# Moving slot products, a gather and the sort behind the products that free weight tiles (one-core mixture-of-experts layer)

## Chip, cores and metric

One core of one Trainium2 chip runs the whole layer in one program. The metric is the device time of one execution in microseconds. The kernel before takes 644.44 us, the median of three runs (643.93 to 645.47).

## What is computed

The reference is one layer of a trunk for 128 context tokens and 128 latent tokens: a mixer of attention and mLSTM heads, and then a mixture of 64 experts of which each token takes 8. Only the second half matters here:

```
gate   = one_hot(top-8 of 64 experts) * normalised sigmoid scores     # per token
a      = silu(t @ w_gate[e]) * (t @ w_up[e])                          # 1024 -> 256, each expert
routed = sum over e of (a * gate[e]) @ w_down[e]                      # 256 -> 1024
y      = x + g2 * (routed + shared expert)
```

All in float32. The weights of one expert are three matrices of 1 MB, and all 64 experts are read: 192 tiles of 1 MB, most of the 252.55 MB that the kernel moves.

## The kernel before

**Stages.** Up to about 160 us the kernel computes modulation, projections, attention, the mLSTM and the output projection. Then it normalises, scores the experts, and starts on the experts at about 180 us. The experts are what the change is in.

**Experts.** Each expert has 64 slots for tokens (32 for those with few tokens). A step takes two experts (PAIR) or four (QUAD) whose slots fill 128 rows, and a group is two steps, called par 0 and par 1. `two_steps` writes the work of PE for a group, in this order:

1. `gate_up` of par 0 (line 1265): slots times `w_gate` of the step, then times `w_up`, into bank 6.
2. `combine` (L1282) of the step before: its expert outputs are added to the tokens.
3. `activations_turned` (L1348): the product is transposed, DVE copies it to `actT` (L2313).
4. `slots_to_tokens` (L1245), here "slot product": two small matrix products that tell for each slot its token and its gate. DVE's `turned` (L2303, L2305) takes them over into `ptone` and `gslot` and signals `t_copied`.
5. `down` of par 0 (L1341): `actT` times `w_down`, in two halves, into banks 5 and 4. ACT (`yhi`, L1740) and DVE (`ylo`, L2325) empty them.
6. `gate_up` of par 1, then `combine` of par 0.
7. The next group's tokens are gathered in four products (`gather`, L1236, quarters q 0 to 3) into banks 7, 4, 5, 7. ACT copies each to `xe` (L1722, `gathered`) and signals `x_copied`. The transposes of par 1 stand behind the first quarter.
8. The slot product of the next group's par 0 into bank 6, then `down` of par 1.

Before it writes banks 5 and 4, `down` of par 1 waits until the third quarter has been copied out of bank 5 (`x_copied` of `group * 4 + 7`).

In the first group the sort of the experts by their number of tokens is added. `turn_slots` (L1356 to L1360) finds the order, SP reads it before the tiles from the third group on, and `sort_slots` (L1366) permutes the slot tables, which `sorted_out` on DVE takes over. The sort stands between the slot product and `down` of par 0.

**Weight tiles.** The 192 tiles are loaded by SP's queue in one fixed order, each into a place that an earlier tile leaves. There are 16 places, one of them used once, so that tile number g waits for the tile 15 or so before it. SP waits for a semaphore that PE sets at the end of a product: `gate_used` (after the product with `w_gate`), `e_filled` (after `w_up`), `y_filled` (after the second half of `down`). In what follows:

- tiles 19 and 20 wait for `down` of step 0,
- tiles 25 and 26 for `down` of step 1,
- tiles 27 to 30 for the products with `w_gate` and `w_up` of step 2,
- tiles 33 and 34 for the gates of step 3, tiles 35 and 36 for its `w_up`,
- tiles 37 and 38 for `down` of step 3,
- tiles 39 to 42 for the gates of step 4, the first QUAD step.

The groups are PAIR, PAIR, then twice (QUAD, four times PAIR), then QUAD.

The waits in `down` and `gate_up`, and the order at the end of a group:

```
pe.wait_ge(x_copied, group * 4 + (3 if opening else 4))   # gate_up, par 0
pe.wait_ge(t_copied, n + 1)
...
pe.wait_ge(a_copied, n + 1)                               # down, first half
if par == 1 and not last:
    pe.wait_ge(x_copied, group * 4 + 7)
```

Of the kernel before, what the change touches and what calls it, by code (L numbers as in the profile page):

```python
# [14 lines left out]
P = 128  # L15
NST = 2
# [28 lines left out]
PAIR, QUAD = 2, 4  # L45
# [44 lines left out]
def build(nc, t, o, overflow_at=CAP):  # L90

    ctx = ExitStack()
    with ctx:
# [200 lines left out]
        sil = sb("sil", [P, FE], where=late)  # L294
        act_e = sb("act_e", [P, FE], where=late)
        actT = sb("actT", [P, JF, 2 * CAP], where=late)
        over_y = ExitStack()
        slots_turned = sb("slots_turned", [NE, 4, P], where=over_y)
        over_y.close()
        over_y = ExitStack()  # L300
        over_yhl = sb("over_yhl", [P, EW], where=over_y)
        over_y.close()
# [178 lines left out]
            return unit + par if kind == QUAD else unit  # L481

        FIRST_BANKS = (7, 0, 3, 4)
        G2_BANKS = ((7, 4), (4, 5))
        FINAL = (slice(512, 1024), slice(256, 512), slice(0, 256))
        FINAL_BANK = (5, 4, 7)
# [331 lines left out]
        def _(pe):  # L818
# [418 lines left out]
                                 pone[:, s, :, :].rearrange("p a b -> p (a b)"), start=(i == 0), stop=(i == 3))  # L1237
                ins.then_inc(x_filled, 1)

            def slots_to_tokens(kind, par, e, gates):  # L1240

                ps = bank[6 - 2 * par]
                for s in range(NST):
                    one = pone[:, s, 2 * par:2 * par + 2, :].rearrange("p a b -> p (a b)").bitcast(F32)
                    ins = mm(ps[:, 0:2 * kind], one, gates[:, s, bass.ds(e, kind), :].rearrange("p e a -> p (e a)"),  # L1245
                             start=(s == 0), stop=(s == 1))
                ins.then_inc(t_filled, 1)

            def gate_up(kind, par, n, unit, group, again, spread=False):

                w = P // kind
                opening = not again and unit == 0
                if par == 0:
                    pe.wait_ge(x_copied, group * 4 + (3 if opening else 4))
                    pe.wait_ge(t_copied, n + 1)
                for part in range(2):
                    for j in range(kind):
                        weights_ready(pe, kind, par, part, j, unit, again)
                    for k in range(KD):
                        if opening and par == 0 and part == 0 and k == 6:  # L1260
                            pe.wait_ge(x_copied, group * 4 + 4)
                        for j in range(kind):
                            weights = weights_of(kind, par, part, j, unit, again).rearrange("p (k f) -> p k f", k=KD)
                            slots = slice(par * P + j * w, par * P + (j + 1) * w)
                            ins = mm(bank[6][j * w:(j + 1) * w, part * FE:(part + 1) * FE], xe[:, k, slots],  # L1265
                                     weights[:, k, :], start=(k == 0), stop=(k == KD - 1))
                    ins.then_inc((gate_used, e_filled)[part], 1)
                    if spread and part == 0:
                        pe.wait_ge(g2_biased, 1)
                        pe.wait_ge(y_lo, n * 2)  # L1270
                        spread_g2(1)
                        spread_g2(0)
# [96 lines left out]
            def two_steps(kind, e, n, group, unit, following, gates=gate_s, before=True, starts=False, shared=None, ends=False,  # L1369
                          again=False):  # L1370

                last = following is None
                gate_up(kind, 0, n, unit, group, again)
                if before:
                    combine(1, n - 1, more=int(again))
                if starts:
                    turn_slots()
                activations_turned(n)
                slots_to_tokens(kind, 1, e + kind, gates)
                if starts:  # L1380
                    sort_slots()
                down(kind, 0, n, unit, group, last, again)

                if shared == "gate":
                    shared_gate()
                elif shared == "rest":
                    shared_up()
                gate_up(kind, 1, n + 1, unit, group, again, spread=ends)
                if starts:
                    pe.wait_ge(sorted_ready, 1)  # L1390
                    pe.wait_ge(cnt_ready, 1)
                combine(0, n, starts, halves=(0,) if ends else (0, 1), more=int(again))
                if shared == "gate":
                    pe.wait_ge(sg_copied, 1)
                elif shared == "rest":
                    pe.wait_ge(sact_ready, 1)
                if not last:
                    gather(0, group + 1)
                activations_turned(n + 1)
                if ends:  # L1400
                    combine(0, n, halves=(1,))
                if not last:
                    for q in range(1, 4):
                        gather(q, group + 1)
                if shared == "rest":
                    shared_down()
                pe.wait_ge(a_copied, n + 2)
                if not last:
                    slots_to_tokens(following, 0, e + 2 * kind, gate_s)
                if ends:  # L1410
                    down_final(unit)
                else:
                    down(kind, 1, n + 1, unit, group, last, again)

            def first_round():
                gather_first()
                evacuated(pe, "counts")
                gather(2, 0)
                pe.wait_ge(gate_ready, 1)
                pe.wait_ge(token_ids, 2 * NST)  # L1420
                slots_to_tokens(PAIR, 0, 0, gate)
                gather(3, 0)
                two_steps(PAIR, 0, 0, 0, 0, PAIR, gates=gate, before=False, starts=True)
                two_steps(PAIR, 4, 2, 1, 1, QUAD)
                for it in range(TURNS):
                    two_steps(QUAD, 24 * it + 8, 10 * it + 4, 5 * it + 2, 6 * it + 2, PAIR, shared=("gate", "rest")[it])
                    for i in range(4):
                        two_steps(PAIR, 24 * it + 16 + 4 * i, 10 * it + 6 + 2 * i, 5 * it + 3 + i, 6 * it + 4 + i,
                                  PAIR if i < 3 else QUAD)
                two_steps(QUAD, NE - 8, STEPS - 2, GROUPS - 1, NE // 4 - 2, None, ends=True)  # L1430
# [25 lines left out]
        def _(act):  # L1456
# [268 lines left out]
            def pair(par, n_pair, group, last=False, starts=False, ends=False, more=0):  # L1725
                act.wait_ge(e_filled, n_pair + 1)
                A(sil[:, :], bank[6][:, 0:FE], ACT.Silu).then_inc(e_silu, 1)  # L1727
                if starts:
                    act.wait_ge(turns_filled, 1)
                    A(slots_turned[:, :, :].rearrange("p a b -> p (a b)"), bank[1][0:NE, :], ACT.Copy).then_inc(turns_copied, 1)  # L1730
                if par == 1 and not last:
                    gathered(group + 1)
                if ends:
                    for i in range(N_FINAL):
                        act.wait_ge(y_filled, n_pair * 2 + (i + 1))
                        A(act_e[:, :] if i == 2 else final_y(yhi, i), final_out(i), ACT.Copy, scale=gslot[:, par:par + 1]).then_inc(y_hi, 1)
                    return
                for i, n in enumerate((1, 0)):
                    act.wait_ge(y_filled, n_pair * 2 + (i + 1) + more)
                    A(yhi[:, n, :], bank[4 + n][:, :], ACT.Copy, scale=gslot[:, par:par + 1]).then_inc(y_hi, 1)  # L1740

            def shared_gate():

# [48 lines left out]
        def _(dve):  # L1792
# [503 lines left out]
                V.tensor_copy(gate_s[:, :, :, 0], bank[0][:, 2 * NE:4 * NE].rearrange("p (s e) -> p s e", s=NST)).then_inc(sorted_ready, 1)  # L2296
                dve.wait_ge(sorted_ready, 1)

            def turned(kind, par, n):

                ps, w = bank[6 - 2 * par], P // kind
                dve.wait_ge(t_filled, n + 1)
                V.tensor_scalar(ptone[:, par, :], iota[:, :], ps[:, 1:2], None, ALU.is_equal)  # L2303
                for j in range(kind):
                    ins = V.tensor_copy(gslot[j * w:(j + 1) * w, par:par + 1], ps[j * w:(j + 1) * w, 2 * j:2 * j + 1])  # L2305
                ins.then_inc(t_copied, 1)
# [52 lines left out]
                                ALU.mult).then_inc(sact_ready, 1)  # L2359

            def first_round():
                turned(PAIR, 0, 0)
                two_steps(PAIR, 0, 0, PAIR, starts=True)
                two_steps(PAIR, 4, 2, QUAD)
                for it in range(TURNS):
                    two_steps(QUAD, 24 * it + 8, 10 * it + 4, PAIR, shared=(it == 1))
                    for i in range(4):
                        two_steps(PAIR, 24 * it + 16 + 4 * i, 10 * it + 6 + 2 * i, PAIR if i < 3 else QUAD)
                two_steps(QUAD, NE - 8, STEPS - 2, None, ends=True)
# [75 lines left out]
```

## Time and profile before

| | |
|---|---|
| median of three runs | 644.44 us (643.93 to 645.47) |
| span of the profiled execution | 642.9 us |
| median less span | 1.5 us |
| PE busy | 580.9 us (90%) |
| DVE, ACT, POOL busy | 209.8, 168.1, 33.6 us |
| DMA | 252.55 MB, mean 393 GB/s |
| mean granted clock of TensorE | 0.975 |

The profiled execution's own time is known by its span alone, from its first instruction to its last. The times of the three runs lie 1.0 to 2.6 us above this span. Busy shares are means over stages with different limits, and PE's ends are modelled, so a busy PE says little about what bounds a stage.

### The profile page before, as it was taken

Reading aid. Unit: us, or ns where it says so; the run is one execution under the profiler, and the core shown is the slowest. Engines: PE = TensorE matmul, PEld = TensorE weight load, DVE = VectorE, ACT = ScalarE, POOL = GpSimd, SP = SyncE. Lnnn points to the kernel's source line nnn. Section 1 sums busy time; section 2 is a strip of 40 time slices with the busy share of each in tenths; the row PEclk is TensorE's granted clock in tenths of the full one; section 3 lists DMA queues with packets and bytes.
Section 4 is the critical chain, followed back from the end, with each engine's and each line's share of the span. In section 5 each row is a group of like instructions: output and inputs, shape, how many; then the busy total and the mean of one; then the engine's idle time right before and its main releaser. Section 6 shows DMA issues by size and latency. Waiting matters only on the chain.

```text
span 642.9 us, 11139 instructions
## 1 busy us (share of the span) xinstructions
PE 580.9 (90%) x4568; PEld 405.9 (63%) x4568; DVE 209.8 (33%) x474; ACT 168.1 (26%) x309; POOL 33.6 (5%) x79
## 2 busy tenths in 40 slices
PE   0789999999999999989999999587999999998785
PEld 0478777788867676656675757354567676765352
DVE  0287867787832212011212222020121212121103
ACT  3164726672622121111121212010212121212111
POOL 1240210010100000000000000000000000000002
PEclk9989999999999999999999999788999999999879
DMA  8999599989999899999999999999999999999994
GB/s 334 385 339 392 208 363 383 411 317 396 420 378 374 365 415 411 422 422 420 420 421 422 420 420 421 421 422 421 420 422 421 419 421 421 421 421 420 421 399 168
DMA packets 50662, 252.55 MB, mean 393 GB/s; under 512 B 5912, under 2 KB 11680, under 8 KB 26288
## 3 DMA queue, kind: packets, MB, share of 16 engines
q1 hardware_dynamic: 48240, 246.37, 94.5%
q0 software_dynamic: 1840, 4.21, 2.0%
q10 hardware_dynamic: 528, 1.21, 0.5%
q8 instruction: 38, 0.62, 0.4%
q14 instruction: 16, 0.13, 0.1%
HBM read 250.06 MB, written 1.72 MB: 392 GB/s over the span
## 4 chain that ended last, share of the span: by engine, by line
PE 63%; DMA 28%; SPq 3%; ACT 2%; DVE 2%; issue 1%; POOL 0%; POOLq 0%; DVEq 0%; ACTq 0%
PE bank L1265 22%; PE bank L1341 11%; DMA spare<-in_w_up 7%; PE bank L1236 6%; PE bank L1282 5%; DMA xn<-in_w_up 4%; DMA gb<-in_w_down 4%; DMA ring<-in_w_up 4%; DMA ring<-in_w_in 4%; DMA ring<-in_w_mod 2%; PE bank L834 2%; SPq L617 2%; PE bank L876 2%; PE bank L884 2%; PE bank L880 2%; DMA ccol<-in_c 2%
## 5 line engine op out<-in xcount | busy, mean ns | idle before, releaser
L1265 PE MATMUL bank<-ring,xe 128*64 128x256 f32 (+1 forms) x1680 | 179.4, 398 | 22.9 <-DMA ring<-in_w_up 8.2
L1265 PEld LDWEIGHTS bank<-ring,xe 128*64 128x64 f32 (+1 forms) x1680 | 118.0, 131 | 79.3 <-issue 44.8
L1341 PE MATMUL bank<-ring,actT 128*64 128x512 f32 (+1 forms) x368 | 83.6, 617 | 4.2 <-DVE actT L2313 2.1
L2311 DVE TENSOR_TENSOR act_e<-bank,sil 128x256 f32<-128x256 f32 x26 | 11.0, 424 | 188.2 <-ACT sil L1727 188.2
L2325 DVE SCALAR_TENSOR_TENSOR ylo<-bank,gslot,yhi 128x512 fp32r<-128x512 f32 x50 | 37.5, 750 | 83.6 <-ACT yhi L1740 83.6
L1740 ACT ACTIVATE yhi<-bank,gslot 128x512 fp32r<-128x512 f32 x50 | 34.4, 688 | 116.1 <-PE bank L1341 116.1
L1727 ACT ACTIVATE sil<-bank 128x256 f32<-128x256 f32 x26 | 10.0, 385 | 192.1 <-PE bank L1265 192.1
L1236 PE MATMUL bank<-pone,hhi 128*128 128x256 f32 x200 | 50.0, 288 | 0.0
L1341 PEld LDWEIGHTS bank<-ring,actT 128*64 128x64 f32 (+1 forms) x368 | 24.5, 132 | 39.2 <-issue 38.9
L1236 PE MATMUL bank<-pone,hlo 128*128 128x256 f32 x200 | 48.9, 282 | 0.0
L1722 ACT ACTIVATE xe<-bank 128x512 f32<-128x512 f32 x50 | 29.9, 598 | 48.2 <-PE bank L1236 48.2
L1282 PE MATMUL bank<-yhi,ptone 128*128 128x512 f32 x100 | 42.2, 422 | 0.0
L1282 PE MATMUL bank<-ylo,ptone 128*128 128x512 f32 x100 | 39.5, 395 | 0.0
L1236 PEld LDWEIGHTS bank<-pone,hhi 128*128 128x128 f32 x200 | 38.2, 191 | 0.6
L1236 PEld LDWEIGHTS bank<-pone,hlo 128*128 128x128 f32 x200 | 38.1, 191 | 0.6
L1265 PE MATMUL bank<-xn,xe 128*64 128x256 f32 (+1 forms) x160 | 37.9, 392 | 0.0
L1341 PE MATMUL bank<-gb,actT 128*32 128x512 f32 (+1 forms) x56 | 28.8, 662 | 2.1 <-DMA ring<-in_w_down 2.1
L808 POOL TENSOR_TENSOR xn<-xn,xt 128x512 f32<-128x512 f32 (+1 forms) x4 | 4.3, 1106 | 464.5 <-DVE xn L2389 464.5
L1282 PEld LDWEIGHTS bank<-yhi,ptone 128*128 128x128 f32 x100 | 18.7, 187 | 13.1 <-issue 9.8
L1265 PE MATMUL bank<-spare,xe 128*64 128x256 f32 (+1 forms) x112 | 27.0, 397 | 0.0
L445 DVE TENSOR_TENSOR w_rest_over<-ring,w_upper_over 128x4096 fp32r<-128x4096 f32 (+1 forms) x6 | 24.6, 4093 | 7.4 <-ACT w_upper_over L1515 6.0
L876 PE MATMUL bank<-w_upper_over,xhi 128*128 128x512 f32 (+1 forms) x96 | 24.3, 402 | 2.8 <-ACT w_upper_over L1548 2.5
(375 smaller groups left out, 792.0 us busy)
## 6 DMA issues: line engine op xcount, KB each, us to landing
ring<-in_w_gate SPq DMA_DIRECT2D x55, 1024.0 KB, 24.1
ring<-in_w_up SPq DMA_DIRECT2D x50, 1024.0 KB, 25.8
ring<-in_w_down SPq DMA_DIRECT2D x46, 1024.0 KB, 25.8
ring<-in_w_mod SPq DMA_DIRECT2D x12, 2048.0 KB, 13.7
ring<-in_w_in SPq DMA_DIRECT2D x5, 2048.0 KB, 16.1
gb<-in_w_down SPq DMA_DIRECT2D x7, 1024.0 KB, 25.9
gb<-in_w_up SPq DMA_DIRECT2D x5, 1024.0 KB, 21.5
xn<-in_w_gate SPq DMA_DIRECT2D x5, 1024.0 KB, 17.0
```

What stands on the lines that cost most here:

```text
L445: eng.tensor_tensor(proj_rest(c), proj_weights(c), proj_upper(c).bitcast(F32), ALU.subtract).then_inc(first_rest if c == 1 else w_rest, 1)
L617: ins = sp.dma_start(tile(PLACE[g]).rearrange("p (j n) -> p j n", j=JF)[:, :, w], down_dram[e].rearrange("p (j n) -> p j n", j=JF)[:, :, w])
L834: ins = mm(ps[r:r + P // CT, 0:MW], csil[:, CT * a + k, :], w[:, k, MW * c:MW * c + MW], start=(a == 0 and k == 0), stop=(a == 1 and k == ...
L876: mm(ps[s][:, 0:w], xhi[:, k, s * P:s * P + P], proj_upper(c)[:, k, :], start=(k == 0), stop=False)
L880: mm(ps[s][:, 0:w], xlo[:, k, s * P:s * P + P], proj_upper(c)[:, k, :], start=False, stop=False)
L1236: ins = mm(ps[:, k * 256:k * 256 + 256], h[:, s, 2 * q + k, :], pone[:, s, :, :].rearrange("p a b -> p (a b)"), start=(i == 0), stop=(i == 3))
L1265: ins = mm(bank[6][j * w:(j + 1) * w, part * FE:(part + 1) * FE], xe[:, k, slots], weights[:, k, :], start=(k == 0), stop=(k == KD - 1))
L1282: ins = mm(acc[s][n][:, :], ptone[:, par, s * P:s * P + P], y[:, n, :], start=(first and y is yhi), stop=False, skip_group_check=True)
L1341: ins = mm(bank[4 + h][j * w:(j + 1) * w, :], actT[:, f, j * w:(j + 1) * w], weights[:, f, 512 * h:512 * h + 512], start=(f == 0), stop=(f ...
L1722: A(xe[:, 2 * q:2 * q + 2, :], bank[(7, 4, 5, 7)[q]][:, :].rearrange("p (a b) -> p a b", a=2), ACT.Copy).then_inc(x_copied, 1)
L1740: A(yhi[:, n, :], bank[4 + n][:, :], ACT.Copy, scale=gslot[:, par:par + 1]).then_inc(y_hi, 1)
L2325: V.scalar_tensor_tensor(out=ylo[:, n, :], in0=bank[4 + n][:, :], scalar=gslot[:, par:par + 1], in1=yhi[:, n, :].bitcast(F32), op0=ALU.mul ...
```

## The change

Four moves, all in the expert part:

- **First slot product.** In the first group it stood between gathers q=2 and q=3, ahead of the first gates. It now stands behind the products with `w_gate` of step 0 and writes bank 2. The wait for `t_copied` moves to the front of the first `down`.
- **Sort.** `sort_slots` moves from ahead of the first `down` to behind it. Its table `slots_turned` now lies in the place of `sact`, so that it outlives the first `yhi`.
- **Next group's slot product** moves from ahead of `down` of par 1 to behind it.
- **Fourth gather** (q=3) moves behind that slot product. ACT copies it after both `yhi`. The next gates start on three quarters and wait for the fourth at k=6.

DVE's order is unchanged, so that `turned` of the next group stands ahead of both `ylo` of par 1 as before.

```diff
-        over_y = ExitStack()
-        slots_turned = sb("slots_turned", [NE, 4, P], where=over_y)
-        over_y.close()
+        slots_turned = sact[0:NE, :, :].rearrange("p j (a q) -> p (j a) q", a=2)
...
             def gate_up(kind, par, n, unit, group, again, spread=False):
                 if par == 0:
-                    pe.wait_ge(x_copied, group * 4 + (3 if opening else 4))
-                    pe.wait_ge(t_copied, n + 1)
+                    pe.wait_ge(x_copied, group * 4 + 3)
+                    if not opening:
+                        pe.wait_ge(t_copied, n + 1)
...
-                        if opening and par == 0 and part == 0 and k == 6:
+                        if par == 0 and part == 0 and k == 6:
                             pe.wait_ge(x_copied, group * 4 + 4)
...
+                    if opening and par == 0 and part == 0:
+                        pe.wait_ge(gate_ready, 1)
+                        pe.wait_ge(token_ids, 2 * NST)
+                        evacuated(pe, "hb1_0")
+                        slots_to_tokens(PAIR, 0, 0, gate, opening=True)
...
                 if starts:
+                    pe.wait_ge(t_copied, n + 1)
+                down(kind, 0, n, unit, group, last, again)
+                if starts:
                     sort_slots()
-                down(kind, 0, n, unit, group, last, again)
...
                 if not last:
-                    for q in range(1, 4):
+                    for q in range(1, 3):
                         gather(q, group + 1)
                 if shared == "rest":
                     shared_down()
                 pe.wait_ge(a_copied, n + 2)
-                if not last:
-                    slots_to_tokens(following, 0, e + 2 * kind, gate_s)
                 if ends:
                     down_final(unit)
                 else:
                     down(kind, 1, n + 1, unit, group, last, again)
+                if not last:
+                    slots_to_tokens(following, 0, e + 2 * kind, gate_s)
+                    gather(3, group + 1)
...
                 if par == 1 and not last:
-                    gathered(group + 1)
+                    gathered(group + 1, range(3))
...
                     A(yhi[:, n, :], bank[4 + n][:, :], ACT.Copy, scale=gslot[:, par:par + 1]).then_inc(y_hi, 1)
+                if par == 1 and not last:
+                    gathered(group + 1, (3,))
```

**At a group's end.** PE's rows at the end of the first group, of the kernel before. Bank 7 takes the fourth quarter, L1245 is the slot product, L1341 `down`, L1265 the next gates:

```order
L1236 MATMUL bank7<-pone,hhi 128x256
L1236 MATMUL bank7<-pone,hlo 128x256
L1245 MATMUL bank6<-gate_s,pone 128x4 x2
L1341 MATMUL bank5<-ring,actT 64x512 x4
L1341 MATMUL bank4<-ring,actT 64x512 x4
L1265 MATMUL bank6<-xn,xe 64x256
```

The same place in the changed kernel (line 1236 is 1235 there, 1245 is 1244, 1341 is 1346):

```order
L1235 MATMUL bank5<-pone,hhi 128x256
L1235 MATMUL bank5<-pone,hlo 128x256
L1346 MATMUL bank5<-ring,actT 64x512 x4
L1346 MATMUL bank4<-ring,actT 64x512 x4
L1244 MATMUL bank6<-gate_s,pone 128x4 x2
L1235 MATMUL bank7<-pone,hhi 128x256
L1235 MATMUL bank7<-pone,hlo 128x256
```

`down` now follows directly on the third quarter, whose bank 5 it writes. The slot product and the fourth quarter stand between `down` and the next gates.

**The sort.** PE's rows around `down` of step 0, before (L1348 are the transposes, L1366 is `sort_slots`):

```order
L1348 MATMUL bank6<-ident,act_e 128x128 x2
L1245 MATMUL bank4<-gate,pone 128x4 x2
L1366 MATMUL bank0<-place,slots_turned 128x64 x4
L1341 MATMUL bank5<-ring,actT 64x512 x4
L1341 MATMUL bank4<-ring,actT 64x512 x4
```

And changed:

```order
L1353 MATMUL bank6<-ident,act_e 128x128 x2
L1244 MATMUL bank4<-gate,pone 128x4 x2
L1346 MATMUL bank5<-ring,actT 64x512 x4
L1346 MATMUL bank4<-ring,actT 64x512 x4
L1371 MATMUL bank0<-place,sact 128x64 x4
```

Only the slot product is left between the transposes and `down`, and the sort stands ahead of the gates of step 1.

## Rows read from the trace of the kernel before

**Rows 1.** The page, part 2: the span in 40 equal slices.
```profile
GB/s 334 385 339 392 208 363 383 411 317 396 420 378 374 365 415 411 422 422 420 420 421 422 420 420 421 421 422 421 420 422 421 419 421 421 421 421 420 421 399 168
```

**Rows 2.** Stretches: length, busy us of engines, granted clock, DMA share, GB/s.
```profile
180.00:245.00 65.00, 64.69 (x532) 42.85 (x531) 14.24 (x38) 12.72 (x22) 0.00 (x0) 1.00 0.93 381
245.00:300.00 55.00, 50.03 (x471) 33.34 (x465) 10.13 (x25) 8.05 (x14) 0.00 (x0) 1.00 1.01 421
445.00:576.00 131.00, 129.94 (x946) 87.50 (x940) 25.50 (x60) 23.65 (x40) 0.00 (x0) 0.99 1.01 421
```

**Rows 3.** Stretches of 1 us in the opening, the same columns.
```profile
194.00:195.00 1.00, 1.00 (x12) 0.67 (x10) 1.00 (x3) 0.00 (x0) 0.00 (x0) 1.00 0.66 115
195.00:196.00 1.00, 1.00 (x14) 0.64 (x12) 0.73 (x2) 0.00 (x0) 0.00 (x0) 1.00 0.91 385
...
242.00:243.00 1.00, 1.00 (x24) 0.65 (x20) 0.05 (x1) 0.00 (x0) 0.00 (x0) 1.00 0.73 238
```

**Rows 4.** Timeline of SP: start us, us, issue of a tile (19, 25, 37, 39).
```profile
193.17 0.33 SPq L546 DMA_DIRECT2D ring<-in_w_gate  x1
...
210.32 0.88 SPq L546 DMA_DIRECT2D ring<-in_w_gate  x2
...
240.72 0.33 SPq L546 DMA_DIRECT2D ring<-in_w_gate  x1
...
244.32 0.33 SPq L546 DMA_DIRECT2D ring<-in_w_gate  x1
```

**Rows 5.** Timeline of PE at the first group's end.
```profile
205.05 0.28 PE L1236 MATMUL bank<-pone,hhi 128*128 128x256 f32 x1
...
206.01 0.51 PE L1245 MATMUL bank<-gate_s,pone 128*128 128x4 f32 x4
206.45 0.65 PE L1341 MATMUL bank<-ring,actT 128*64 128x512 f32 x2
...
209.93 0.38 PE L1265 MATMUL bank<-xn,xe 128*64 128x256 f32 x1
```

**Rows 6.** Timeline of ACT and DVE there, and ahead of the first QUAD.
```profile
205.25 0.60 ACT L1722 ACTIVATE xe<-bank 128x512 f32<-128x512 f32 x1 [0.36 <-PE bank L1236]
...
206.83 0.32 DVE L2305 COPY gslot<-bank 64x1 f32<-64x1 f32 x2
...
236.44 0.51 PE L1245 MATMUL bank<-gate_s,pone 128*128 128x8 f32 x4
...
237.26 0.65 DVE L2305 COPY gslot<-bank 32x1 f32<-32x1 f32 x4
```

**Rows 7.** Timeline of DVE and PE in step 2: the copy of actT and its waiter.
```profile
219.35 0.42 DVE L2313 COPY actT<-bank 128x256 f32<-128x256 f32 x1 [1.45 <-PE bank L1348]
...
219.92 1.51 PE L1341 MATMUL bank<-ring,actT 128*64 128x512 f32 x6 [0.26 <-DVE actT L2313]
```

**Rows 8.** Timeline of PE and DVE around the first down, and the first slot product.
```profile
178.10 0.51 PE L1245 MATMUL bank<-gate,pone 128*128 128x4 f32 x4
178.47 0.36 PE L1236 MATMUL bank<-pone,hhi 128*128 128x256 f32 x1
...
188.44 1.10 PE L1366 MATMUL bank<-place,slots_turned 64*128 64x64 f32 x8
189.47 3.65 PE L1341 MATMUL bank<-ring,actT 128*64 128x512 f32 x16
192.96 7.08 PE L1265 MATMUL bank<-ring,xe 128*64 128x256 f32 x64
...
188.21 0.42 DVE L2313 COPY actT<-bank 128x256 f32<-128x256 f32 x1 [0.59 <-PE bank L1348]
```

**Rows 9.** The chain that ended last, and PE's waits near the end.
```profile
576.60 26.24 DMA gb<-in_w_down
...
593.04 5.35 PE L1265 MATMUL bank<-ring,xe 128*32 128x256 f32 x64 [2.82 <-DMA ring<-in_w_up]
603.09 0.59 PE L1341 MATMUL bank<-ring,actT 128*32 128x512 f32 x1 [2.06 <-DMA gb<-in_w_down]
```

More of the change, by code:

```diff
@@ L483, in build @@
         FIRST_BANKS = (7, 0, 3, 4)
+        FIRST_SLOTS = 2
         G2_BANKS = ((7, 4), (4, 5))
@@ L1238, in gather, with slots_to_tokens @@
                 ins.then_inc(x_filled, 1)
-            def slots_to_tokens(kind, par, e, gates):
-                ps = bank[6 - 2 * par]
+            def slots_to_tokens(kind, par, e, gates, opening=False):
+                ps = bank[FIRST_SLOTS if opening else 6 - 2 * par]
                 for s in range(NST):
@@ L1418, in first_round @@
                 gather(2, 0)
-                pe.wait_ge(gate_ready, 1)
-                pe.wait_ge(token_ids, 2 * NST)
-                slots_to_tokens(PAIR, 0, 0, gate)
                 gather(3, 0)
@@ L2297, in sorted_out, with turned @@
                 dve.wait_ge(sorted_ready, 1)
-            def turned(kind, par, n):
-                ps, w = bank[6 - 2 * par], P // kind
+            def turned(kind, par, n, opening=False):
+                ps, w = bank[FIRST_SLOTS if opening else 6 - 2 * par], P // kind
                 dve.wait_ge(t_filled, n + 1)
@@ L2361, in first_round @@
             def first_round():
-                turned(PAIR, 0, 0)
+                turned(PAIR, 0, 0, opening=True)
                 two_steps(PAIR, 0, 0, PAIR, starts=True)
```

## Prediction

> **What bounds the kernel now.** I read the slices of the page first, then the stretches, then the seams between DMA and PE in the opening. The slices [rows 1] show the DMA engines full, at 419 to 422 GB/s, from about 257 us until close to the end. The stretches [rows 2] say the same from the other side. From 245 us on the engines move 421 GB/s at a share of 1.01, whether PE is nearly always busy (129.94 of 131 us between 445 and 576) or waits for tiles (50.03 of 55 us). From 180 to 245 us it is different: PE is busy for 64.69 of 65 us and DMA runs at 0.93 and 381 GB/s. There the places for tiles are all taken, and each load waits for PE to finish with an older tile.
>
> So the expert part has two regimes. In the opening PE's releases set when DMA works. After the last gap, the end is that gap's end plus a fixed number of bytes. A microsecond of PE counts only if it moves the last gap or opens a new one. The last gap lies in 242 to 243 us, where 238 GB/s flow instead of 421 [rows 3]: 0.43 us is missing. It is ended by tile 37, which SP issues at 240.72 [rows 4] when `down` of step 3 is done.
>
> How long an issued tile takes to flow is read from the same gaps. Tile 19 is issued at 193.17 [rows 4]. From 194 to 196 the engines move 115 and 385 GB/s [rows 3], which is 1.19 us at 421, so the flow resumes at 194.81: 1.64 us after the issue. Tile 37 by the same 1.64 flows from 242.36, which fits 0.43 us missing behind 242. The Trainium skill says less, in "DMA: Bandwidth & Descriptors", section "Latency and other measured facts": about 600 ns to the first byte for a transfer issued from SP. By that figure tile 37 would have flowed at 241.32, ahead of the queue's end, and there would be no gap; the row shows one, so the measurement decides.
>
> **The parts, one by one.** First the seam at the end of every group but the last.
>
> *What leaves the front of `down`, par 1.* The fourth gather runs from 205.05 to 206.01 and the slot product to 206.45 [rows 5]: 0.96 and 0.44, together 1.40 us.
>
> *What takes its place.* `down` writes bank 5 first, and must wait for ACT's copy of the third quarter. That copy starts at 205.25 and takes 0.60 [rows 6], so it ends at 205.85. PE needs a while to start behind a signal: the copy of `actT` ends at 219.77 and PE starts at 219.92 [rows 7], 0.15 us. `down` starts at 206.00 and not at 206.45. It has **gained 0.45 us, and a stall of 0.95 us is new** (from 205.05). In the kernel before that copy was hidden by the fourth gather and the slot product, and now nothing is left to hide it.
>
> *Behind `down`.* It takes 3.48 us (206.45 to 209.93 [rows 5]), as before; then come 0.44 and 0.96. The next gates start at 206.00 + 3.48 + 1.40 = 210.88, against 209.93: **0.95 us later per group**. Do they wait longer, for `t_copied`? The slot product begins at 206.01 and the last copy to `gslot` ends at 207.15 [rows 5, 6]: 1.14, with the start of PE 1.29, under the 1.40 that the slot product and the fourth gather fill. Ahead of a QUAD group four copies end at 237.91; their slot product begins at 236.44, so 1.47 and 0.15 make 1.62: 0.22 more stall. ACT's copy of the fourth quarter is due at k=6, some 2.6 us into the gates. It starts 0.2 us after the gather and takes 0.60, so it costs nothing. The two `ylo` come after `turned` on DVE and so about 1 us later; their reader, `combine`, stands 7 us of gates away. Their delay costs nothing.
>
> *Sort.* Step 0's copy of `actT` ends at 188.63 [rows 8], so `down` can start at 188.78 instead of 189.47: 0.69 us earlier. Behind it come the 1.03 us of the sort (188.44 to 189.47). The gates of step 1 then start at 188.78 + 3.49 + 1.03 = 193.30 against 192.96: **0.34 us later**, which is the wait for `actT` that the sort used to fill.
>
> *First slot product.* 0.37 us (178.10 to 178.47 [rows 8]) leave the front of the first gates and come back behind them. The gates release their tiles 0.37 us earlier, and from the first `w_up` on PE stands where it stood: 0. The gap near 183 us that it shortens is followed by others, so it brings nothing by itself. DVE takes that product over far ahead of the first `down`.
>
> **The releases.** Adding these shifts in order:
>
> - `down` of step 0: 0.69 earlier.
> - gates of step 1: 0.34 later; `down` of step 1: 0.34 - 0.45 = 0.11 earlier.
> - all of step 2 and the gates of step 3: 0.34 + 0.95 = 1.29 later.
> - `down` of step 3: 1.29 - 0.45 = **0.84 later**.
> - gates of step 4: 1.29 + 0.95 + 0.22 = 2.46 later.
>
> Three of the four releases behind which DMA ran dry come earlier, but the last one comes later, and only that carries through. Tile 25 (issued at 210.32, now 210.21) flows from 211.85. The twelve tiles 25 to 36 take 12 x 1.049 MB / 421 GB/s = 29.9 us, to 241.7. The releases between, 1.29 later, still come before their turn. Tile 37 is issued at 241.56 and flows from 243.20, with two tiles to 248.18. Tile 39, issued at 244.32 [rows 4], is now issued at 246.78 and flows from 248.42: a second gap of 0.24 us. Before, tiles 37 and 38 lasted from 242.36 to 247.34, and tile 39 was there in time. So everything behind is late by 248.42 - 247.34 = **1.08 us**. The four tiles released with those gates last 10 us, so the next release has room.
>
> **After the last gap** PE may fall behind as it likes, while the queue lasts. The deepest cover is read near the end of the second run of PAIR groups: a tile issued at 576.60 lands after 26.24 us [rows 9]. Less 1.64 and its own 2.49, 22 us are queued ahead. PE falls behind DMA by 0.95 us in each of four groups, and 0.22: about 4 us. That is hidden. It meets slack at the end: PE waited 2.82 and 2.06 us for tiles around 593 and 603 [rows 9], and would now wait less. If this cover were gone, those 4 us would show in full.
>
> The sum is +1.08 us. Bounds for the one price with no row of its own, the new stall: from 0.80 (the ACT's 0.20 to start and 0.60, PE at once) to 1.15 (another 0.20 for PE to refill). Each 0.1 us counts twice until step 4, so the sum runs from +0.8 to +1.5. I take 0.95, since the wait for `actT` is the same kind of wait, ahead of the same instruction. On the span that makes 644.0, and on the median, 1.5 above it, 644.44 + 1.08 = **645.5 us**.
>
> **Rivals.**
>
> *The gap at step 4 is wider: slower by over 0.2%.* 0.2% is 1.29 us, about what a measurement of this kernel can tell from no change. It takes a stall of 1.06 us at the end of each of the first two groups in place of 0.95, or a longer wait for `t_copied` ahead of the QUAD. At 1.15 us the time is 645.9, and with 0.3 more at the QUAD 646.2. For it: the margin is 0.1 us. Against it: the durations of ACT's copy hardly vary.
>
> *The stall is short.* If `down` comes 1.0 us or more earlier, three releases move forward and the last gap goes: at a stall of 0.4, `down` of step 3 comes 0.34 + 0.4 - 1.00 = 0.26 earlier, 644.2 us. Against it stands the fixed 0.60 of the copy. Faster by 0.2% would need no stall at all and more.
>
> *Tiles flow sooner after their issue.* The flow starts 0.6 us behind the issue, as that figure of the skill has it. As a mechanism here: tile 37 at 242.16 would follow the queue without a gap worth naming, tile 39 at 247.38 too, and the time would stay at 644.4 to 644.6. The gaps behind tiles 19 and 37 [rows 3] speak against it.
>
> *PE's lag empties the queue.* In a run of four PAIR groups PE loses 4 us, and if the queue held less than that the end would be up to 4 us later, 648 to 650. The 22 us queued speak against it.
>
> **Numbers.** The forecast has 0.50. A wider gap has 0.28 (645.8 to 646.6), a short stall 0.10 (644.0 to 644.7), sooner flow 0.05, an emptied queue 0.03, a gain that I don't see 0.04. The forecast itself lies 0.2 us inside the bound of 1.29, so about a seventh of it falls beyond. Slower: 0.28 + 0.03 + 0.06, about 0.37. Faster: 0.05. Same: 0.58. The range from 643.9 to 646.9 leaves out the emptied queue and most of the gains.
>
> **What would show it.** Right: `down` of par 1 waits for ACT's `xe` in nearly every group, 0.8 to 0.95 us each, about 10 us in all; tile 37 issued near 241.6; a gap of about 1.5 us before 243.2; PE waiting less for DMA later; 421 GB/s from 250 us on. Wrong: tile 37 issued at or before 240.7, no wait on `xe`, or DMA below 415 GB/s in a PAIR run.

## The result and the profile after

The changed kernel takes 647.27 us, the median of six runs (646.07 to 649.71). The kernel before, run with it, takes 645.11 (643.93 to 646.3). The ratio is **1.0044, with a 95% interval of 1.003 to 1.0058**: 2.8 us slower, between 1.9 and 3.7. The forecast was 645.5 us and "the same within 0.2%", in a range to 646.9. It was wrong: the direction held, and the size was 2.6 times too small.

The profiled execution has a span of 644.3 us and took 646.07 us, the shortest of the six. Its page, parts 1 and 2, against [rows 1]:

```profile
span 644.3 us, 11139 instructions
PE 581.8 (90%) x4568; PEld 406.7 (63%) x4568; DVE 208.7 (32%) x474; ACT 168.1 (26%) x309; POOL 33.6 (5%) x79
...
GB/s 329 387 340 391 214 364 384 411 339 398 419 349 383 371 379 387 423 422 420 420 421 421 420 422 422 420 421 420 421 420 420 422 422 420 422 420 422 420 398 178
```

From the seventeenth slice on both pages read 419 to 423 GB/s, up to the last two. The fifteenth and sixteenth read 379 and 387 against 415 and 411. The twelfth differs too, 349 against 378, but the next two win part of that back (383 and 371 against 374 and 365). The loss lies ahead of 258 us, as forecast.

The two executions don't reach the experts at the same moment. The first product of the first gather starts at 175.18 before and at 174.22 after, 0.96 us earlier, in a part that the change doesn't touch. So times of the expert part are compared from that product on. The stretches below are counted from there, 4 to 52, 52 to 100 and 100 to 400 us behind it; first of the kernel before, then of the changed one (columns as in [rows 2]):

```profile
179.18:227.18 48.00, 47.69 (x363) 31.29 (x363) 11.06 (x30) 8.86 (x15) 0.00 (x0) 1.00 0.91 370
227.18:275.18 48.00, 46.92 (x486) 31.51 (x485) 8.56 (x25) 9.76 (x17) 0.00 (x0) 1.00 1.01 417
179.18:275.18 96.00, 94.60 (x845) 62.80 (x847) 19.62 (x55) 18.62 (x32) 0.00 (x0) 1.00 0.96 394
275.18:575.18 300.00, 281.40 (x2124) 189.49 (x2118) 57.10 (x135) 49.74 (x84) 0.00 (x0) 0.98 1.01 421
```

```profile
178.22:226.22 48.00, 46.65 (x345) 30.06 (x346) 10.97 (x32) 8.87 (x15) 0.00 (x0) 1.00 0.93 367
226.22:274.22 48.00, 45.44 (x468) 31.88 (x468) 8.26 (x22) 8.47 (x15) 0.00 (x0) 1.00 1.00 396
178.22:274.22 96.00, 92.08 (x809) 61.94 (x812) 19.24 (x53) 17.34 (x30) 0.00 (x0) 1.00 0.96 382
274.22:574.22 300.00, 281.12 (x2110) 186.91 (x2104) 55.66 (x136) 50.52 (x86) 0.00 (x0) 0.99 1.01 421
```

This is a ledger of bytes. Over 96 us the changed kernel moves 12 GB/s less, which at 421 GB/s is 12 x 96 / 421 = **2.7 us of transfer missing**. In the 300 us that follow nothing is lost and nothing is won back. The span grew by 1.4 us only, since this execution started the experts 0.96 us earlier: from that first product to the end it is 2.4 us longer. The six runs tell the 2.8 us.

What PE waited for in the changed kernel, without the two long waits that lie ahead of the experts (engine, line, who ended the wait: us in total, times, longest):

```profile
...
PE bank L1346 <- ACT xe L1727: 7.8, 10, 0.8
PE bank L1265 <- DMA ring<-in_w_gate: 6.2, 1, 6.2
PE bank L1346 <- DMA ring<-in_w_down: 5.5, 2, 4.0
PE bank L1265 <- DMA ring<-in_w_up: 4.2, 2, 3.1
...
```

The wait in the first line is new: ten waits for ACT's copy of 0.78 us each. PE's timeline and ACT's and SP's at the first group's end, beside [rows 4 to 6]:

```profile
204.71 0.28 PE L1235 MATMUL bank<-pone,hlo 128*128 128x256 f32 x1
205.76 3.65 PE L1346 MATMUL bank<-ring,actT 128*64 128x512 f32 x16 [0.78 <-ACT xe L1727]
209.35 0.61 PE L1244 MATMUL bank<-gate_s,pone 128*128 128x4 f32 x4
209.81 0.36 PE L1235 MATMUL bank<-pone,hhi 128*128 128x256 f32 x1
...
210.94 0.43 PE L1265 MATMUL bank<-xn,xe 128*64 128x256 f32 x1
```

```profile
205.02 0.60 ACT L1727 ACTIVATE xe<-bank 128x512 f32<-128x512 f32 x1 [0.36 <-PE bank L1235]
```

```profile
209.63 0.34 SPq L545 DMA_DIRECT2D ring<-in_w_gate  x1
...
241.30 0.33 SPq L545 DMA_DIRECT2D ring<-in_w_gate  x1
...
246.58 0.33 SPq L545 DMA_DIRECT2D ring<-in_w_gate  x1
```

The last fence has the issues of tiles 25, 37 and 39. With the 0.96 us added, they stand at 210.59, 242.26 and 247.54 against 210.32, 240.72 and 244.32 [rows 4]: 0.27, 1.54 and 3.22 us later. The forecast had 0.11 earlier, and 0.84 and 2.46 later.

### The profile page after: what moved, and what is told of

Its sections match the earlier page's. It is cut to its first block, busy times and chain, and to the rows that moved or that the text cites. A ratio compares the mean times of both kernels' runs of the same rounds, so it can differ in the third digit from the quotient of the medians.

```text
span 644.3 us, 11139 instructions
## 1 busy us (share of the span) xinstructions
PE 581.8 (90%) x4568; PEld 406.7 (63%) x4568; DVE 208.7 (32%) x474; ACT 168.1 (26%) x309; POOL 33.6 (5%) x79
## 4 chain that ended last, share of the span: by engine, by line
PE 68%; DMA 20%; ACT 4%; SPq 3%; DVE 2%; issue 1%; POOL 0%; POOLq 0%; DVEq 0%; ACTq 0%
PE bank L1265 22%; PE bank L1346 11%; PE bank L1235 6%; PE bank L1287 6%; DMA xn<-in_w_up 4%; DMA ring<-in_w_up 4%; PE bank L833 4%; DMA gb<-in_w_down 4%; DMA spare<-in_w_up 4%; PE bank L875 2%; PE bank L883 2%; PE bank L879 2%; SPq L616 2%; DMA ccol<-in_c 2%; DMA ring<-in_w_down 1%; DMA ring<-in_w_in 1%
## 5 line engine op out<-in xcount | busy, mean ns | idle before, releaser
L1265 PE MATMUL bank<-ring,xe 128*64 128x256 f32 (+1 forms) x1680 | 175.2, 388 | 13.5 <-DMA ring<-in_w_gate 6.2
L1265 PEld LDWEIGHTS bank<-ring,xe 128*64 128x64 f32 (+1 forms) x1680 | 116.1, 128 | 61.0 <-issue 24.9
L1346 PEld LDWEIGHTS bank<-ring,actT 128*64 128x64 f32 (+1 forms) x368 | 26.4, 133 | 46.6 <-issue 46.6
L2332 DVE SCALAR_TENSOR_TENSOR ylo<-bank,gslot,yhi 128x512 fp32r<-128x512 f32 x50 | 36.4, 748 | 50.4 <-ACT yhi L1745 50.0
L1235 PE MATMUL bank<-pone,hhi 128*128 128x256 f32 x200 | 51.3, 292 | 0.0
L2310 DVE TENSOR_SCALAR ptone<-iota,bank 128x256 fp32r<-128x256 f32 x26 | 9.3, 358 | 89.0 <-PE bank L1244 89.0
L1265 PE MATMUL bank<-xn,xe 128*64 128x256 f32 (+1 forms) x160 | 36.4, 381 | 0.0
```

Source lines behind the costliest of these rows:

```text
L1235: ins = mm(ps[:, k * 256:k * 256 + 256], h[:, s, 2 * q + k, :], pone[:, s, :, :].rearrange("p a b -> p (a b)"), start=(i == 0), stop=(i == 3))
L1346: ins = mm(bank[4 + h][j * w:(j + 1) * w, :], actT[:, f, j * w:(j + 1) * w], weights[:, f, 512 * h:512 * h + 512], start=(f == 0), stop=(f ...
L2332: V.scalar_tensor_tensor(out=ylo[:, n, :], in0=bank[4 + n][:, :], scalar=gslot[:, par:par + 1], in1=yhi[:, n, :].bitcast(F32), op0=ALU.mul ...
```

## The experiments

All ratios are to the kernel before on the same chip, with 95% intervals. "Ledger" is the transfer missing in the 96 us from 4 us behind the first gather's first product, worked out as above, against the 394 GB/s of the kernel before; its last digit is 1 GB/s, or 0.2 us. One profile of each kernel stands behind it, so 0.2 us is also what it can tell: the control e12, which moves nothing, has a ledger of 0.2.

The variants are made from the changed kernel by putting parts back. Two small things of it stay in all of them, e12 too: the table of the sort lies in the place of `sact`, and the next gates start on three quarters. e12's tiles 37 and 39 are issued within 0.02 us of the kernel before, counted from the first gather.

### One part at a time

**e1_opening_only.** The change with the sort and the groups' ends put back:

```diff
-                down(kind, 0, n, unit, group, last, again)
                 if starts:
                     sort_slots()
+                down(kind, 0, n, unit, group, last, again)
...
-                    for q in range(1, 3):
+                    for q in range(1, 3 if "g" in how else 4):
```

`how` is an empty text here, so that the loop runs over three quarters as before.

> Only the first slot product is moved. In the changed kernel's trace it costs 0.7 us behind the first gates against 0.37 ahead of them, so PE stands 0.25 to 0.3 us later from the first w_up on. Theory A (only PE's releases around the last DMA gap near 243 us count): down of step 3 is released 0.25 us later, +0.3 us in all (ratio 1.000 to 1.001). Rival C (the two opening moves carry most of the 2.8 us): +1 us or more (1.0015 or more).

Measured: 0.9994 (0.9976 to 1.0011), ledger 0.2 us. That fits theory A, and the 1 us or more of rival C is out for this move.

**e2_sort_only.** The kernel before with the change's order of `down` and `sort_slots` in the first group.

> Only the sort is moved behind the first down. Down of step 0 releases 0.7 us earlier, all that follows 0.35 to 0.5 later. Theory A: +0.3 to +0.5 us (1.0005 to 1.001). Rival C: +1 us or more.

Measured: 1.001 (0.9996 to 1.0023), ledger 0.7 us. Tile 37 is issued at 239.98, 66.06 us behind the first gather's start at 173.92. Before it was 240.72 - 175.18 = 65.54. So the sort's move costs 0.52 us of PE, not 0.34. The ratio alone can't tell it from nothing, and its interval reaches 1.5 us; that the 1 us of rival C is out for the sort rests on the ledger.

**e3_ends_early and e4_ends_late.** The groups' ends of the change, chosen by group. `how` says what stands behind `down`: `s` the slot product, `g` the fourth gather. e3 has both at the ends of the first two groups and neither later, e4 the other way round:

```diff
+                how = EARLY if not again and group in (0, 1) else LATE
                 if not last:
-                    for q in range(1, 4):
+                    for q in range(1, 3 if "g" in how else 4):
                         gather(q, group + 1)
...
+                if not last and "s" in how:
+                    slots_to_tokens(following, 0, e + 2 * kind, gate_s)
+                if not last and "g" in how:
+                    gather(3, group + 1)
```

> The slot product and fourth gather stand behind down only at the ends of the first two groups; opening and sort as before. Theory A: this carries most of the loss: gates of step 2 about 1.3 us later, those of step 4 about 2.6 later, +1.5 to +2.5 us (1.0023 to 1.004). Rival B (PE's lag in the ten later groups costs the time): within 0.5 us of before.

> The same, but only at the ends of the third to the twelfth group. PE stalls about 0.8 us for ACT's xe in nine of them. Theory A: the DMA queue stays full at 421 GB/s and covers it, within 0.5 us of before (0.9992 to 1.0008). Rival B: +1.5 us or more (1.0023 or more).

Measured: **two ends at the front cost 1.0032 (1.0013 to 1.0051), ten behind them 1.0009 (0.9996 to 1.0023)**. The early ones have a ledger of 1.6 us, the late ones of 0.2. With the 0.2 and 0.7 of e1 and e2 that makes the 2.7 us of the whole change. The same stretches, of e3 first and then of e4:

```profile
179.13:275.13 96.00, 93.85 (x829) 63.44 (x831) 19.31 (x54) 17.93 (x31) 0.00 (x0) 1.00 0.96 387
275.13:575.13 300.00, 280.31 (x2108) 186.99 (x2102) 57.28 (x135) 50.41 (x85) 0.00 (x0) 0.97 1.01 421
```

```profile
180.62:276.62 96.00, 93.34 (x833) 61.42 (x835) 18.91 (x51) 18.02 (x31) 0.00 (x0) 1.00 0.97 393
276.62:576.62 300.00, 282.55 (x2098) 188.89 (x2092) 56.37 (x138) 50.38 (x85) 0.00 (x0) 0.98 1.01 421
```

And PE's waits in the two, of e3 from 180 to 250 us and of e4 from 250 to 600 us:

```profile
PE bank L1341 <- ACT xe L1727: 1.6, 2, 0.8
```

```profile
PE bank L1341 <- ACT xe L1727: 6.2, 8, 0.8
```

Two waits, 1.6 us in all, come with the loss. Eight waits, 6.2 us in all, leave no mark that the runs can tell: the queue is deep there, and the stretch that holds them stays at 421 GB/s. e4's interval just reaches the 1.5 us of rival B; the 421 GB/s, and e11 below, put it out.

### Without the stall, and with less behind `down`

**e5_banks.** The change with another bank for two of the gathers, so that `down` doesn't wait for the copy ahead of its first half:

```diff
-                ps = bank[(7, 4, 5, 7)[q]]
+                ps = bank[((7, 4, 5, 7) if first else (7, 5, 4, 7))[q]]
...
                         if par == 1 and not last:
-                            pe.wait_ge(x_copied, group * 4 + 7)
+                            pe.wait_ge(x_copied, group * 4 + 6)
                     elif par == 0:
                         pe.wait_ge(t_copied, n + 2)
+                    elif not last:
+                        pe.wait_ge(x_copied, group * 4 + 7)
```

> The changed kernel with the second and third gathers' banks exchanged (7, 5, 4, 7), so that down writes first the bank that was copied long ago and waits for the third quarter's copy only ahead of its second half. The stall for ACT's xe (0.78 us at each end) should be gone. Theory A (stall and lag before the last DMA gap): gates of step 2 about 1.2 us later than before and not 2.0, gates of step 4 about 1.7 and not 3.2; it should win back 2 us or more of the changed kernel's 2.8 (ratio to before 0.9995 to 1.001). Rival D (the waits on the copy don't matter, the extra PE switches do): 1.003 or more as before.

Measured: 1.0024 (1.0009 to 1.0039). The stall is gone from the waits, but the kernel is still 1.6 us slower than before (0.6 to 2.5), where 0.6 at most was expected. The expectation of 2 us won back is a miss. The interval overlaps that of the change, so how much was won back isn't shown. Its profile, with a ledger of 3.2 us, says little of the size: in that execution TensorE ran at half its clock ahead of the experts (last section), and PE was some 1.5 us late (its tile 16 comes 9.20 us behind the first gather's start, that of the change 7.69) before anything that the change moves.

**e7_ends_banks.** The ends of the change with these banks, opening and sort as before.

> Both pieces behind down, banks exchanged, opening and sort as before. Each end about 0.35 us longer, down of par 1 ends 1.3 us earlier: down of step 3 releases about 0.9 us earlier, down of step 1 1.3 earlier. Theory A: the gap near 243 us goes, -0.5 to -1.0 us (0.9985 to 0.9992). Rival D: no gain.

Measured: 1.0017 (1.0006 to 1.0028), slower, where 0.5 to 1 us of gain was expected. This is the run that broke the prediction's sum. SP's issues of tiles 37 and 39:

```profile
239.41 0.33 SPq L545 DMA_DIRECT2D ring<-in_w_gate  x1
...
244.68 0.33 SPq L545 DMA_DIRECT2D ring<-in_w_gate  x1
```

The first gather starts at 174.73 there. So tile 37 comes 64.68 us behind it, 0.86 us **earlier** than before (65.54), just as meant. Tile 39 comes at 69.95 against 244.32 - 175.18 = 69.14, 0.81 later. By the sum's rule the two together are a gain: tiles 37 and 38 end 0.86 earlier, tile 39 flows 0.3 us behind their end, and everything behind is 0.6 us early. The stretches show another thing: ahead in the first half, behind in the second.

```profile
178.73:226.73 48.00, 47.69 (x359) 30.91 (x359) 10.98 (x30) 8.86 (x15) 0.00 (x0) 1.00 0.93 375
226.73:274.73 48.00, 44.50 (x462) 30.62 (x462) 7.75 (x21) 8.47 (x15) 0.00 (x0) 1.00 1.00 405
```

375 against 370 GB/s is 0.6 us won, 405 against 417 is 1.4 us lost; over the whole 96 us it is 390 against 394, a ledger of 0.9 us.

**e6_gather_behind.** Only the fourth gather behind `down`; the slot product stays ahead of it, with the banks of before. **e8_gather_banks** is the same with the banks exchanged.

> Only the fourth gather stands behind down; the slot product stays ahead of it and covers 0.44 us of the copy; opening and sort as before. Theory A: stall 0.4 us, each end 0.5 to 0.7 us longer, gates of step 4 1.0 to 1.4 us later, which is within the 1.4 us that tile 39 had in hand; down of step 3 about 0.1 later: +0.0 to +0.5 us (1.000 to 1.0008). Rival D: half of the full ends' loss or more, 1.0015.

> Only the fourth gather behind down, banks exchanged: no stall for the copy and one switch less than e7. Down of step 3 releases 0.7 to 0.9 us earlier. Theory A: -0.5 to -0.9 us (0.9986 to 0.9992). Rival D: no gain.

Measured: 1.0022 (1.0009 to 1.0035) and 1.0017 (1.0002 to 1.0032), ledgers 1.8 and 0.5 us. What theory A expected is missed in both, in the same direction as in e7. In e8 tile 37 is 0.6 us earlier than before and tile 39 0.5 later, as in e7, and both kernels are slower. In e6 they are 0.4 and 1.5 us later, which leaves tile 39 0.2 us in hand. Given these issue times, the sum's rule makes e6 0.4 us later and e8 0.6 us earlier. The numbers of rival D, the extra switches of PE, do fit e6, e7 and e8. But the switches are in the issue times already, and by the rule those give no such loss. That led to the next question: what is a tile's lead worth?

### The price of being late, by itself

Eight spare products of a gather's size ahead of chosen gates of the kernel before; nothing reads what they compute:

```diff
                     pe.wait_ge(t_copied, n + 1)
+                    if not again and group == 2:
+                        for _ in range(1):
+                            for i in range(8):
+                                mm(bank[6][:, 0:256], hhi[:, i % 2, i, :], pone[:, i % 2, :, :].rearrange("p a b -> p (a b)"),
+                                   start=True, stop=True)
```

**e9_late_step4** has them ahead of step 4 as shown, **e10_late_step2** with `group == 1`, ahead of step 2, and **e11_late_deep** with `group in (4, 5, 6)`.

> The kernel before, with eight spare products (128x256, the size of one gather, about 0.96 us of PE) ahead of the gates of step 4. Nothing is computed from them. Tile 39 is released 0.96 us later, tile 37 as before. Theory E (the sum of the prediction: a tile has 1.4 us in hand and flows at 421 GB/s): no loss, 0.9993 to 1.0007. Theory F (a tile that comes just in time flows slowly behind a nearly empty queue, so that lead is lost gradually): +0.4 to +1.2 us, 1.0006 to 1.002.

> The same eight products ahead of the gates of step 2: all of PE from step 2 on is 0.96 us later, tiles 37 and 39 too. Theory E: +1.0 us (1.0015). Theory F: +1.2 to +2 us (1.002 to 1.003), the whole lag and a slower flow. Theory B (an early lag is hidden by the queue as a late one): within 0.4 us.

> The same eight products ahead of the first gates of the fifth, sixth and seventh groups, 2.9 us of PE in all, where some 20 us of transfers are queued. Theories E and F: no loss, 0.9993 to 1.0007. Theory B: +1 us or more.

| | PE made later | measured | in us | ledger |
|---|---|---|---|---|
| e9 | ahead of step 4 | 1.0015 (1.0001 to 1.003) | 1.0 (0.1 to 1.9) | 2.1, clock disturbed |
| e10 | ahead of step 2 | 1.0033 (1.0018 to 1.0049) | 2.1 (1.2 to 3.2) | 1.4 |
| e11 | three times, deep in the queue | 0.9996 (0.9983 to 1.001) | -0.3 (-1.1 to 0.6) | 0.2 |

e10's issues of tiles 37 and 39, behind a first gather at 174.16:

```profile
241.02 0.33 SPq L546 DMA_DIRECT2D ring<-in_w_gate  x1
...
244.63 0.33 SPq L546 DMA_DIRECT2D ring<-in_w_gate  x1
```

66.86 and 70.47 against 65.54 and 69.14: the spare products made PE 1.3 us later, not 0.96. The sum's rule gives 1.3 us for that, the ledger has 1.4, and the interval of the runs includes it. So e10 doesn't tell theories E and F apart.

e9 does, if narrowly. It costs 1.0 us, with an interval that just leaves out zero, where theory E, the rule of the prediction's sum, gives none. In its profile TensorE's clock fell ahead of the experts (last section) and made everything 1.5 us late, so the first half of its ledger (359 GB/s) says nothing of the change. The second half can be read. Its issues of tiles 37 and 39, and the flow behind tile 37:

```profile
241.71 0.33 SPq L546 DMA_DIRECT2D ring<-in_w_gate  x1
...
246.46 0.33 SPq L546 DMA_DIRECT2D ring<-in_w_gate  x1
```

```profile
244.00:248.00 4.00, 4.00 (x80) 2.39 (x76) 0.00 (x0) 0.00 (x0) 0.00 (x0) 1.00 1.01 416
248.00:252.00 4.00, 4.00 (x45) 2.78 (x37) 0.42 (x1) 0.38 (x1) 0.00 (x0) 1.00 0.98 352
```

They are 4.75 us apart, against 3.60 before. So tile 39 is 1.15 us later against tile 37, and by the rule it still has 0.2 us in hand: it flows from 246.46 + 1.64 = 248.10, and tiles 37 and 38 last to 248.33. And just there the flow falls to 352 GB/s, which is 0.7 us of transfer.

Three delays of the same kind cost nothing where the queue is deep. e11's stretch from 300 to 385 us has PE busy nearly throughout and no byte lost:

```profile
300.00:385.00 85.00, 84.20 (x609) 58.31 (x609) 16.83 (x42) 15.96 (x27) 0.00 (x0) 1.00 1.01 421
```

**e12_banks_only**, the control: the banks exchanged and nothing moved.

> The kernel before with the banks of the second and third gather exchanged, nothing moved. PE waits for that copy in neither kernel, so this is a control: 0.9993 to 1.0007 by every theory; what it shows beyond is the noise of such a comparison.

Measured: 1.0001 (0.9988 to 1.0014). The exchange of banks by itself does nothing that shows, and a comparison of this size tells differences of about 0.13%.

Where the flow is lost is seen in the changed kernel from 224 to 235 us, between two of the old gaps:

```profile
224.00:226.00 2.00, 2.00 (x20) 1.44 (x18) 1.03 (x2) 0.69 (x1) 0.00 (x0) 1.00 1.02 426
226.00:231.00 5.00, 5.00 (x50) 3.99 (x48) 0.73 (x2) 0.00 (x0) 0.00 (x0) 1.00 0.92 272
231.00:235.00 4.00, 4.00 (x28) 3.26 (x25) 0.60 (x2) 0.80 (x2) 0.00 (x0) 1.00 1.00 420
```

Tile 31 is issued there at 224.66, 50.4 us behind the first gather's start, and 48.4 before (223.60 - 175.18). By the sum it came just at its turn: tiles 25 to 30 flow from 209.63 + 1.64 = 211.27 and last 15 us, to 226.2, and tile 31 flows from 226.3. The engines count as busy for 0.92 of the five microseconds and move 272 GB/s: (421 - 272) x 5 / 421 = 1.8 us of transfer are missing in a stretch that looks full by its share.

e6 and e10 show the same place. Tile 31 is issued at 224.95 and 223.89 there and has 0.4 us in hand by the sum. Three microseconds of each, e6 first:

```profile
226.00:229.00 3.00, 3.00 (x30) 2.42 (x28) 1.02 (x2) 0.00 (x0) 0.00 (x0) 1.00 0.90 276
226.00:229.00 3.00, 3.00 (x31) 2.40 (x28) 0.00 (x0) 0.00 (x0) 0.00 (x0) 1.00 0.86 276
```

This first loss is not what makes the change dearer than its sum. The sum has a gap of about 1.6 us ahead of tile 37, which ends when tile 37 is released; the loss uses it up, and from 235 to 243 us the engines move 421 GB/s. The same holds for e10, whose whole loss is that of the rule. What comes on top is lost behind tile 37, which is issued at 241.30 and flows from 242.94. The changed kernel there:

```profile
243.00:252.00 9.00, 9.00 (x139) 6.54 (x132) 1.50 (x3) 0.74 (x2) 0.00 (x0) 1.00 0.99 367
```

(421 - 367) x 9 / 421 = 1.2 us are missing, where the rule has 0.3 for the second gap. What makes the engines slow in such a stretch is not shown; that they are slow where tiles come just in time, and not where they are queued, is.

## Why the prediction was wrong

**What bounds the kernel: right.** The bytes are lost ahead of 260 us, and behind it both kernels run at 421 GB/s. e4 and e11 show PE's lag hidden there, as forecast with the 22 us queued.

**The new stall: right, within 0.02 us.** PE's next product would have stood at 204.83, and `down` starts at 205.76: 0.93 where 0.95 was forecast, in ten groups, 7.8 us of idle time against "about 10". The wait for ACT's copy of the third quarter is the mechanism.

**The end of a group: under-sized.** Forecast 0.95 later, measured 1.3. In e3, whose start is the same within 0.05 us, the gates of step 2 release tile 27 at 215.01 against 213.76 before. Most of the missing 0.35 shows where PE changes between kinds of products, which the sum moved at no cost. `down` takes 3.59 and not 3.48 (205.76 to 209.35), and the fourth gather, now between the slot product and the gates, 1.13 and not 0.96 (209.81 to 210.94).

**The opening's slot product: forecast 0, measured 0.25 to 0.3.** It leaves a place between two gathers, which are products of its own kind, and comes between two runs of 64-row products. The gates' own release does come 0.44 earlier, and brings nothing, as forecast.

**The sort: forecast 0.34, measured 0.52** (e2). The same reason is likely and wasn't tested.

**The stall ahead of the QUAD: over-sized.** Forecast 0.22 more; the slot product to the first gate takes 1.59 us in the first group (209.35 to 210.94) and 1.68 ahead of step 4.

Together they put tiles 37 and 39 at 1.54 and 3.22 us later. The prediction's own rule, fed with these, gives: tile 39 flows from 247.54 + 1.64 = 249.18, against 247.34 before, 1.8 us. So of the 2.7 us in the ledger, **1.1 was the forecast, 0.8 is PE's under-sized lag, and 0.9 is the rule itself**.

**The step that failed** is the one called "The releases", by 0.9 us, besides the terms above that were too small by 0.8. There a tile was taken as in time if it flows, 1.64 us behind its issue, before the queue ends, and the queue to run at 421 GB/s until then. Tile 39 "was there in time" with 1.4 us in hand, and "the releases between, 1.29 later, still come before their turn". The runs show that a tile with a few tenths in hand already costs flow. e9 and e6 leave tile 39 0.2 us by this rule: e9 costs 1.0 us (0.1 to 1.9) where the rule gives none, and e6 costs 1.4 us (0.6 to 2.3) where it gives 0.4. e7 costs 1.1 us (0.4 to 1.8) where it gives a gain of 0.6. In the changed kernel 1.2 us are missing behind tile 37 in place of 0.3. Where tile 39 keeps its 1.4 us to tile 37, the rule holds: with the issue times of e1, e2 and e10 it gives 0.3, 0.5 and 1.3 us, and their ledgers are 0.2, 0.7 and 1.4. How much a tile needs in hand, between 0.4 and 1.4 us, no run shows. Why the flow is slow stays open.

**The rivals.** The one given 0.28, a wider second gap, named the right side and the wrong cause: it wanted a longer stall and topped out at 646.6, while the stall was as forecast. "Tiles flow sooner after their issue" is out: in the changed kernel tile 25 is issued at 209.63 with the queue empty, and 74 and 229 GB/s flow from 210 to 211 and to 212. That is 0.72 us at 421, so the flow resumes at 211.28, 1.65 us behind the issue.

```profile
210.00:211.00 1.00, 1.00 (x10) 0.87 (x10) 0.95 (x4) 0.15 (x1) 0.00 (x0) 1.00 0.59 74
211.00:212.00 1.00, 1.00 (x11) 0.71 (x12) 1.00 (x2) 0.60 (x1) 0.00 (x0) 1.00 0.60 229
```

A short stall, made in e7 and e8, releases tile 37 earlier as forecast, and doesn't speed the kernel up. "PE's lag empties the queue" is out by e4 and e11. None of the variants beats the kernel before; e1 at 0.9994 can't be told from it.

## What to carry to other kernels

A product moved behind the one that frees a buffer is paid twice: by the wait that it used to hide, and by the lead of every later release. Before such a move, ask for each release in the stretch where the queue is short how much it has in hand afterwards, and not only for the one where the queue runs dry: here a few tenths of a microsecond were not enough. Where the queue is deep the same order cost nothing that the runs can tell, so the move could be judged by its first two groups alone.

Price moved products by their neighbours: a small product between products of another shape took 0.1 to 0.3 us more here than among its own kind.

## What the runs showed of the hardware

DMA's busy share can read nearly full while bytes are missing: 0.92 at 272 GB/s for five microseconds of the changed kernel, 0.90 and 0.86 at 276 GB/s for three of e6 and e10, against 1.01 at 421 where tiles are queued. In a stretch where tiles come just in time, read the GB/s.

The engine clock can shift the part under study. In two of the fourteen profiles, e5's and e9's, TensorE's granted clock fell ahead of the experts. In e5, in stretches of 2 us:

```profile
172.00:174.00 2.00, 1.56 (x12) 1.04 (x10) 1.72 (x8) 0.38 (x1) 0.00 (x0) 1.00 0.96 397
174.00:176.00 2.00, 1.34 (x10) 1.37 (x11) 2.00 (x6) 0.00 (x0) 0.00 (x0) 0.91 1.05 438
176.00:178.00 2.00, 2.00 (x11) 2.00 (x11) 1.83 (x11) 0.75 (x3) 0.00 (x0) 0.50 0.99 414
178.00:180.00 2.00, 2.00 (x15) 2.00 (x13) 0.05 (x1) 1.06 (x3) 0.00 (x0) 0.73 1.03 430
```

PE had two short idle times here, behind DVE, and the clock then stood at 0.50, the lower level of 1.2 GHz, before it returned to 1.00 by 180 us. The other twelve profiles have the same idle times and stay at 1.00. The gathers took longer, and the first tiles were released some 1.5 us later. That is more than most of the effects tried here, so a single profile of the opening can't be set against another before its clock is read.
